# The order of operations in a chunked RWKV-7 core on Trainium2: weight rounding, residual sums, head sums and projection blocks in other places

## The reference, cut to what matters

```python
def rwkv7_step(state, inp):
    r, w, k, v, a, bb = inp
    sa = jnp.einsum('bhij,bhj->bhi', state, a)
    state = (state * w[:, :, None, :] + sa[..., None] * bb[:, :, None, :]
             + v[..., None] * k[:, :, None, :])
    y = jnp.einsum('bhij,bhj->bhi', state, r)
    return state, y
...
    _, y = lax.scan(rwkv7_step, state0, xs)
    y = jnp.moveaxis(y, 0, 1)
    mu = jnp.mean(y, axis=-1, keepdims=True)
    var = jnp.mean(jnp.square(y - mu), axis=-1, keepdims=True)
    y = ((y - mu) * lax.rsqrt(var + GN_EPS)).reshape(b, s, RWKV_WIDTH) * ln_w + ln_b
    bonus = jnp.sum(rh * kh * r_k, axis=-1, keepdims=True) * vh
    return (y + bonus.reshape(b, s, RWKV_WIDTH)) * g
...
        mixed = jnp.concatenate([attn.reshape(b, s, ATTN_WIDTH), rw], axis=-1).astype(h.dtype)
        h = h + mixed @ w_out[l]
```

## Time and profile before

| | us |
|---|---|
| median of 3 runs | 2189.42 (2188.83 to 2189.79) |
| the profiled execution | 2188.19 |
| its span, from the first to the last instruction | 2186.5 |
| TensorE busy | 2125.9 (97%) |
| VectorE busy | 1541.6 (71%) |
| ScalarE busy | 1033.4 (47%) |

### The profile page before, as it was taken

One profiled execution on the slowest core, in us unless ns is written; L12 is line 12 of the kernel. 1 busy time (PEld: TensorE's weight loads), 2 busy tenths in 40 slices (PEclk: granted clock), 3 DMA queues, 4 the chain that ended last, 5 costly groups with the idle time before them and its releaser, 6 DMA issues.

```text
span 2186.5 us, 51663 instructions
## 1 busy us (share of the span) xinstructions
PE 2125.9 (97%) x20608; PEld 2072.9 (95%) x20608; DVE 1541.6 (71%) x2015; ACT 1033.4 (47%) x1342; POOL 267.5 (12%) x178
## 2 busy tenths in 40 slices
PE   7999999999999999999999989899999999999997
PEld 7999999999999999999999888799999999999997
DVE  7889999999645668768877666576666666654544
ACT  6544444444454445556344444654444444444443
POOL 0354444444200000100011000000000000000000
PEclk9999999999999999999999999999999999999999
DMA  7555555555565555555655211255656565556664
GB/s 265 185 171 180 180 182 187 185 184 182 195 193 193 192 201 202 188 184 166 210 180 192 88 51 60 74 188 184 194 192 196 191 195 192 193 187 197 188 191 139
DMA packets 107106, 387.84 MB, mean 177 GB/s; under 512 B 12032, under 2 KB 12160, under 8 KB 106752
## 3 DMA queue, kind: packets, MB, share of 16 engines
q1 hardware_dynamic: 104400, 375.44, 52.5%
q0 software_dynamic: 2176, 9.78, 1.3%
q10 hardware_dynamic: 432, 1.21, 0.1%
HBM read 384.29 MB, written 2.10 MB: 177 GB/s over the span
## 4 chain that ended last, share of the span: by engine, by line
PE 77%; DVE 14%; issue 4%; ACT 3%; DMA 1%; DVEq 0%; SPq 0%; ACTq 0%
PE ps_main L1700 24%; PE ps_main L1701 23%; PE ps_main L1702 23%; DVE w_lo L990 6%; ACT w_hi L503 2%; DVE m L1149 1%; DVE m L1150 1%; PE ps_aux L2055 1%; DVE acc L1156 1%; DMA w_raw<-wmain 1%; DVE g_scan L1159 0%; PE ps_main L2026 0%; PE ps_aux L1942 0%; PE ps_aux L1773 0%; PE ps_main L2027 0%
## 5 line engine op out<-in xcount | busy, mean ns | idle before, releaser
L990 DVE TENSOR_TENSOR w_lo<-w_raw,w_hi 128x1024 fp32r<-128x1024 f32 x718 | 917.8, 1295 | 429.1 <-ACT w_hi L503 421.7
L503 ACT ACTIVATE w_hi<-w_raw 128x1024 fp32r<-128x1024 f32 x718 | 748.4, 1048 | 717.2 <-PE ps_main L1702 656.5
L1700 PE MATMUL ps_main<-xs,w_hi 128*128 128x256 f32 x1664 | 463.2, 278 | 7.7 <-DVE w_lo L990 6.7
L1701 PE MATMUL ps_main<-xs,w_hi 128*128 128x256 f32 x1664 | 460.2, 277 | 0.0
L1702 PE MATMUL ps_main<-xs,w_lo 128*128 128x256 f32 x1664 | 460.2, 277 | 0.0
L1700 PE MATMUL ps_main<-x3s,w_hi 128*128 128x256 f32 x1408 | 389.3, 276 | 0.0
L1701 PE MATMUL ps_main<-x3s,w_hi 128*128 128x256 f32 x1408 | 388.8, 276 | 0.0
L1702 PE MATMUL ps_main<-x3s,w_lo 128*128 128x256 f32 x1408 | 388.8, 276 | 0.0
L1700 PEld LDWEIGHTS ps_main<-xs,w_hi 128*128 128x128 f32 x1664 | 312.8, 188 | 16.1 <-DVE w_lo L990 11.2
L1702 PEld LDWEIGHTS ps_main<-xs,w_lo 128*128 128x128 f32 x1664 | 312.6, 188 | 0.0
L1701 PEld LDWEIGHTS ps_main<-xs,w_hi 128*128 128x128 f32 x1664 | 312.4, 188 | 0.0
(11 more groups left out here) (422 smaller groups left out, 3722.7 us busy)
## 6 DMA issues: line engine op xcount, KB each, us to landing
w_raw<-wmain SPq DMA_DIRECT2D x622, 512.0 KB, 3.5
w_raw<-wdown SPq DMA_DIRECT2D x80, 512.0 KB, 3.7
w_raw<-wdown SPq DMA_DIRECT2D x16, 256.0 KB, 2.7
bias<-bias POOLq DMA_DIRECT2D x8, 384.0 KB, 3.4
x_res<-xt POOLq DMA_DIRECT2D x4, 512.0 KB, 7.2
out<-x_res SPq DMA_DIRECT2D x3, 512.0 KB, 2.8
x_first<-xt SPq DMA_DIRECT2D x2, 512.0 KB, 7.1
x_first<-xt ACTq DMA_DIRECT2D x2, 512.0 KB, 9.9
```

What stands on the lines that cost most here:

```text
L503: nc.scalar.activation(whi[:, s, 0:width], raw[:, s, 0:width], ACT.Copy).then_inc(hi_ready, 1)
L990: V.tensor_tensor(wlo[:, s, 0:width], raw[:, s, 0:width], whi[:, s, 0:width].bitcast(F32), ALU.subtract)\
L1700: nc.tensor.matmul(out, whi[:, s, w], high[:, k, :], start=(first and kk == 0), stop=False)
L1701: nc.tensor.matmul(out, whi[:, s, w], low[:, k, :], start=False, stop=False)
```

## The change

Nothing is added to the arithmetic and nothing is taken from it. Instructions stand in another order, and three results lie in other banks.

- On ScalarE the high part of the unit in the middle of a chunk is rounded ahead of the copy of md, no longer behind it. In chunk 0 the first `wout_hi` stands behind the copy of n4t, no longer ahead of n2t. The copy of x stands behind that of n8.
- On VectorE a residual sum (`wout_add`) now stands ahead of a split (`wout_lo`) in each place: behind n2, behind t1, and at a chunk's end. In the middle of the chunk the split comes right behind the copy of q2. The first split of a chunk stands behind the copy of n4.
- The head sum of the former chunk stands behind the first pair of products and vt, no longer ahead of the pair, and goes to a bank of main (that of the next free column). `centre` follows n2 and a residual sum.
- On TensorE w2 stands ahead of both halves of x, and x's second half behind the pair w4 and n8. w2, w4 and w8 go to B, B and C, x to A.
- TensorE's blocks: 2, 3, 3 in the first part of a chunk become 2, 4, 4 in chunk 0 and, in the others, none, 4, 4 (the second head sum stands in the place of the 2). The product of the gate with y is done ahead of the product with the root (`gated`). The copy of sa stands ahead of `rest`.
- PART goes from (4, 4, 4, 2, 2) to (4, 4, 3, 2, 3): chunk 2 has 24 blocks, no longer 32, and behind the core there are 24, no longer 16. Of these 4 stand ahead of the last head sum, 5 between the two sums and 15 behind; before it was 0, 6 and 10.
- Behind the core the Ln table is loaded (`gg`) ahead of `square`, no longer behind it, and the last low part of the recurrence is made ahead of a split, no longer behind it.

```diff
-        PART = (4, 4, 4, 2, 2)
+        PART = (4, 4, 3, 2, 3)
...
                 exchanged("q", mat["n"])
+                wout_hi()
                 exchanged("md", mat["md"])
-                wout_hi()
...
                 take("n2", mat["n2"])
-                if not i:
-                    gate_bonus(0)
-                wout_lo()
                 if i:
                     wout_add()
-                take("n4", mat["n4"])
+                    centre(i - 1, main[:, first_column(i) % 2, :])
+                    take("n4", mat["n4"])
+                else:
+                    gate_bonus(0)
+                    take("n4", mat["n4"])
+                wout_lo()
...
                 done("t1", V.tensor_tensor(mat["n2t"][:, :, :], mat["nt"][:, :, :], eye, ALU.add))
+                wout_add()
                 if not i:
                     gate_bonus(1)
                 take("q2", mat["n4"])
                 wout_lo()
-                wout_add()
...
+                if i:
+                    c = first_column(i)
+                    pe.wait_ge(wa_free[c % 2], c // 2)
+                    sum_heads(vr[:, :, toks(i - 1)], main[:, c % 2, :])
                 dv("n2")
                 ac("n2t")
                 two(("n4", "n2t", "n2"), ("n4t", "n2", "n2t"))
                 ac("vt")
+                prod("w2", "n2", "w")
+                dv("n4")
                 by_halves(OUT["x"], lambda j, h: (ba[hrow(h), j, toks(i)], state[hrow(h), j, :])).then_inc(x_half, 1)
-                dv("n4")
-                prod("w2", "n2", "w")
-                pe.wait_ge(x_half, i + 1)
-                done("x", second_halves(OUT["x"], lambda j, h: (ga[hrow(1 - h), h, j, :], st[hrow(1 - h), j, h, :])))
                 ac("n4t")
                 dv("w2")
                 two(("w4", "n4", "w"), ("n8", "n4t", "n4"))
-                ac("x")
+                pe.wait_ge(x_half, i + 1)
+                done("x", second_halves(OUT["x"], lambda j, h: (ga[hrow(1 - h), h, j, :], st[hrow(1 - h), j, h, :])))
+                dv("w4")
...
+            wout(4)
             pe.wait_ge(core_act, NCH * len(AC))
             sum_heads(vr[:, :, toks(NCH - 1)], aux[:, 3, :])
-            wout(6)
+            wout(5)
             pe.wait_ge(gn_sq, NCH)
             sum_heads(gsq[:, :, :], aux[:, 2, :])
-            wout(10)
+            wout(15)
```

More of the change, by code:

```diff
@@ L883, in core @@
                 exchanged("n4t", mat["n4t"])
+                if not i:
+                    wout_hi()
+                exchanged("n8", mat["n2"])
                 copy("x", xv)
-                exchanged("n8", mat["n2"])
                 act.wait_ge(core_mm, i * len(MM) + MM["bkt"] + GO)
@@ L911, in core @@
                     .then_inc(core_act, 1)
-                if not last:
-                    wout_hi()
+                for _ in range(PART[i] - 2):
                     wout_hi()
@@ L1437, in masked_products, with diagonal_t @@
                 return V.tensor_tensor(r[:, h, :, :], both[:, :, CH:P], m[:, :, CH:P], ALU.mult)
[L1439 to L1442, removed]
+            def diagonal_t(h):
+                return V.tensor_tensor(mat["nt"][hrow(h), :, :], ga[hrow(h), h, :, :], mask("mdiagt", h), ALU.mult)
             def diagonal(banks):
@@ L1478, in gate_bonus, with centre, gated @@
                     ins.then_inc(gate_mixed, 1)
-            def centre(i):
+            def centre(i, sums):
                 dve.wait_ge(gn_mm, 2 * i + 1)
                 t = vr[:, :, tokens(i)]
-                V.scalar_tensor_tensor(t, aux[:, 3, :].rearrange("p (j n) -> p j n", n=CH), -1.0 / 64, t, ALU.mult, ALU.add)\
+                V.scalar_tensor_tensor(t, sums.rearrange("p (j n) -> p j n", n=CH), -1.0 / 64, t, ALU.mult, ALU.add)\
                     .then_inc(gn_mean, 1)
+            def gated(i):
+                dve.wait_ge(gn_sq, i + 1)
+                for c in range(2):
+                    half = vr[:, 4 * c:4 * c + 4, tokens(i)]
+                    ins = V.tensor_tensor(half, half, gsb[c][:, :, tokens(i)], ALU.mult)
+                link(ins)
             def group_out(i):
@@ L1557, in chunk @@
                 if not last:
+                    diagonal_t(0)
                     mm("g2")
                     done("gm1", masked_products(1, G2, grs[(i + 1) % 2]))
-                    diagonal_t()
+                    diagonal_t(1)
                     mm("n")
                     diagonal(OUT["n"])
-                    done("nf", rest(OUT["n"]))
                 mm("sa")
@@ L1566, in chunk @@
                 if not last:
+                    done("nf", rest(OUT["n"]))
                     done("w1", V.tensor_tensor(mat["w"][:, :, :], mat["nt"][:, :, :], eye, ALU.add))
                     if i:
+                        gated(i - 1)
                         group_out(i - 1)
@@ L2094, in _ @@
                     pe.wait_ge(gate_sb, 4)
-                wout(2)
+                    wout(2)
+                else:
+                    pe.wait_ge(gn_sq, i)
+                    c = first_column(i) + 1
+                    pe.wait_ge(wa_free[c % 2], c // 2)
+                    sum_heads(gsq[:, :, :], main[:, c % 2, :])
                 ac("n8")
+                prod("w8", "n2", "w")
                 if i:
[L2098 to L2102, removed]
+                    pe.wait_ge(gn_mean, i)
+                wout(4)
                 dv("w8")
+                ac("x")
+                two(("qt", "f", "w"), ("q", "w", "f"))
                 if i:
                     pe.wait_ge(gn_var, i)
-                two(("qt", "f", "w"), ("q", "w", "f"))
-                wout(3)
+                wout(4)
                 dv("qt")
@@ L2134, in _ @@
                 done("sa", every_head(OUT["sa"], lambda j, h: (mat["n2"][hrow(h), j, :], xv[hrow(h), j, :])))
-                wout(3 if not last else 2)
+                wout(3 if not last else 1)
                 dv("sa")
```

45 lines of the change are left out of this document (23 added, 22 removed).

## The result

The changed kernel takes 2173.76 us (median; 2172.1 to 2181.3), the kernel before in the same comparison 2189.6: a ratio of 0.9933, 95% interval 0.9921 to 0.9944. The forecast was 2172.9. So 15 to 16 us are gone.

A forecast was written before the change was run, and what follows sets the result against it. TensorE, busy 97%, was taken as the bound, so only waits, switches and clock count: waits 21.4 to 6.9, less 0.6 for switches, plus 1.5 and 1.7 clock, 17.1, taken as 16.5, giving 2172.9 us; range 2170.5 to 2177.

The forecast's parts named there:

- The walk: Prediction's wait-by-wait reckoning of the new order in the stage from 1242 to 1407 us: TensorE's waits from 21.4 to 6.9.
- issue wait: TensorE wait of 0.8 us for "issue", taken as no part of the order and staying; if gone, 0.8 more saved.
- rival (a): The clock falls in chunk 0 behind two new waits, 0.6 and 2.2, costing 1.5 to 1.7: 2174.5 us; chance 0.22.
- m_w in chunk 0: Chunk 0's start: the split waits for w_hi on ScalarE, so TensorE gets a new wait of 2.2 us.
- m_w in chunks 1 to 3: Start of these chunks: w2 before x and a split ahead of m_w; each waits 0.67 where 0.2 stood, 2.0 us.
- rwkv_l: Wait at woutb's start behind the core: chain shorter, more blocks over it, so 3.2 us falls to 0.3.
- m_n4t: Waits in the middle of the chunks: 6.1 us before, 0.1 left in chunk 0 and 0.2 in chunk 3.
- The Ln table ahead of the square: Table load moved earlier behind the core: valued at nothing; by the skill page's figures 0.3 us at most.
- 0.6 for the switches: Head sum between small products in chunks 1 to 3: shape switches cost 0.2 us each, 0.6 in all.
- 1.5 + 1.7: Clock falls regained: 1.5 us in chunk 3 and 1.7 at woutb's start, bringing 13.9 saved to 17.1.
- rival (c): In woutb VectorE leaves more sums and splits behind the core, taking 2 to 3 us back: 2175.5; chance 0.08.
- 16.5 taken: Total saving used for the profiled execution: 17.1 us lowered because the walk came out 0.5 too long on the kernel before.

The follow-up runs named there:

- middle alone: Kernel before with w_hi rounded ahead of md and the residual sum ahead of the copy of q2: ratio 0.9983, distance between the two TensorE marks 168.27 us.
- end alone: Kernel before with PART (4, 4, 3, 2, 3), blocks 4, 5, 15, table and gate products ahead, last low part ahead of a split: ratio 0.9972.
- kernel with the old end: Changed kernel with PART and the blocks (0, 6, 10) as before: 2177.31 us, ratio 0.994.
- split moved in chunk 0 alone: Changed kernel with the first split of a chunk behind w2's sum in chunk 0 only: 2173.93 us, ratio 0.9921.
- version with the split moved: Changed kernel with the split behind the copy of n4 put behind w2's sum in every chunk: 2173.82 us, then 2170.0 with more runs.
- kernel with middle and end: Kernel before with the moves in the middle of a chunk and those behind the core, without the starts of the chunks: 2177.69 us, ratio 0.9937.

## Why the prediction was right, and where it was not

**The bound and the waits: right.** The walk forecast woutb's start near 1391, 1392 with the issue wait; it is at 1392.64 with a fall of the clock in front of it that the forecast left to rival (a). Term by term, forecast and measured: m_n2t in chunk 0 0.6 and 0.50; m_w in chunk 0 2.2 and 2.17; m_w in chunks 1 to 3 0.67 each and 0.61, 0.61, and in chunk 2 an issue wait of 0.5 in its place; stack 0.5 and 0.32; mt's copy, for which sa waits, 0.3 and 0.34; md 0.35 and 0.2; rwkv_l 0.3 and 0.27; m_n4t 0.3 in all and no wait of 0.25 or more. No wait for x_res or rkv, as forecast. (The rows before have 26 waits, where the prediction counts 25; that is worth 0.1.)

**Each part.** That the middle alone takes m_n4t's waits away, that the end alone brings woutb from 3.18 to under 0.5, and that the blocks behind the core cover the copy of y are shown by the experiments. The Ln table ahead of the square was valued at nothing: in the kernel with the old end woutb waits 2.15 where the walk, with nothing for the table, has 2.0. The forecast's 0.6 for the switches was not measured by itself.

**The clock: half right.** "With the clock, 1.5 + 1.7, it is 17.1" took both falls as gone and no new one. Both are gone, and each went with its own wait (middle alone, end alone). But rival (a), given 0.22, is what happened, in all three traces. The argument against it, that waits of 1.4 and 1.5 had not ended in a fall, was weak, since the new wait was 2.2 with one of 0.5 ahead of it, more than the 0.5 and 1.7 of chunk 3 that did. Across the traces: the five with a wait of this size at that place (1.3 with 0.6 for issue, 1.6 with 0.35, 1.9 to 2.2) have the fall; the eight without it (four of them with 1.4 for m_n2t, one with 0.57 left for m_w) have none there. So the fall needs the wait. That it always comes with it is not shown: behind a wait of 2.2 elsewhere in the same kernels it came in eight traces of thirteen (last section). The fall costs about 1.6, an estimate: with the split moved in chunk 0 alone 3.8 were saved, and the wait was 2.2. The Trainium skill (TensorE: Matmul & The Clock Gate, Part 1) says that the moment of a change of clock varies from run to run. The traces agree for that other place: where the clock falls there, it does so between 0.3 before the wait's end and 1.6 behind it; in chunk 0 it is 0.0 to 0.8 behind it.

**woutb: the step that failed.** The sum has 1.7 for the clock at woutb's start and takes the rest of woutb as it was. The 1.7 came in (1.6) and was taken back by the slower spacing of its matmuls, 1.9. It is not rival (c), which had VectorE as the bound: no wait stands there. The forecast had no such case. In the three traces of the changed kernel it is there twice (325 matmuls in 38 us) and once not (337), and it is in none of the other ten traces; so the median of the changed kernel probably holds some of it, and a part of what separates it from the version with the split moved may be that. Whether the order has to do with it, at so few traces, is not settled.

So the number was right within 1 us, in part by luck: the stage without its fall was 0.6 better than forecast (13.9 and 1.5 against 14.8), the fall cost 1.5 and woutb 1.9. The profiled execution gained 13.7, 2.8 less than the 16.5 taken; that the median gained 15.8, 2.1 more than the profiled pair, lies in differences between executions of the same code (last section), which the forecast did not have.

**A better order.** With the split behind w2's sum the distance is 5.4 shorter, in two traces. In the medians it is 2170.0 against 2175.06 on one chip (0.9909 of the kernel before against 0.9928); the comparison on the other chip, of four runs, had 0.9927 and does not show it.

## What to carry over

Where an engine's work can't shrink, write down for each wait the chain that ends it and the work that covers it, and walk the new order before running it: here the distances of nine kernels came out within about 1 us of such a walk, once it was known where the clock falls. A product moved earlier needs its whole chain moved, the other work in its engine's queue included: w2 went ahead of x on TensorE and a split was left in its way on VectorE, which cost 5.4 of the 21 us that were to be had (19.3 in the distance, 1.6 at woutb's start), about 1.6 of them for the clock. Price a new wait of about 2 us with a fall of the clock behind it that is likely though not certain, and compare kernels by a distance between two marks in the trace rather than by medians when a few us are at stake.

## What the runs showed of the hardware that was not expected

**Two spacings of the same matmul.** A 128x256 product of woutb or the large projections starts 113.3 or 117.8 ns behind the one before it at full clock, hardly ever in between, and can keep to one value for hundreds of matmuls. In some places a part of them is slow in every trace, as at 1050 to 1100 us; others are slow only in some traces, as the stretch at 850 to 900 us, where both kernels here have the same code. The version with the split moved, second trace, and the kernel with middle and end:

```profile
850.00:900.00 50.00, 50.00 (x444) 1.00 0.63 201
```
```profile
850.00:900.00 50.00, 50.00 (x427) 1.00 0.60 189
```

The second kernel has 2376 slow steps ahead of the stage where the first has 1416: 960 at 4.5 ns, 4.3 us, in work that no edit touches, and its traced execution took 2181.0 where its median is 2177.7. The three traces with that stretch slow reach the mark at 1236.8 to 1238.3 us, the other ten at 1231.1 to 1235.3. So it is a main part of the spread ahead of the stage; executions without a trace can't be looked into. Inside the distance the same counts are 34 to 156 slow steps, at most 0.6 us of it. What sets the value was not found.

**Falls of the clock behind short waits.** Each fall lasted some 3.4 us at 1.2 GHz; the two that could be priced from differences, in chunk 0 and at woutb's start, cost 1.6 us each. In chunk 0 they followed the wait for m_w (1.3 to 2.2, the shorter ones with an "issue" wait ahead) in five traces of five, and in chunk 3 a wait of 1.7 in two of two; the waits of 1.4 and 1.5 in chunks 0 to 2 were not followed by one. A wait of 3.18 at woutb's start was, both times, and one of 2.15 there, in the kernel with the old end, was not. Near 825 us, in work that no edit touches, all thirteen traces have a wait of 2.2 for the tile ms, and a fall came in eight of them. The version with the split moved, first and second trace:

```profile
824.53 0.38 PE L1714 MATMUL ps_main<-ms,w_hi 128*128 128x256 f32 x1 [2.26 <-DVE ms L1243]
...
826.00:828.00 2.00, 2.00 (x11) 0.50 0.71 236
```
```profile
826.07 0.38 PE L1714 MATMUL ps_main<-ms,w_hi 128*128 128x256 f32 x1 [2.26 <-DVE ms L1243]
...
826.00:828.00 2.00, 1.93 (x14) 1.00 0.79 262
```

The code and the wait are the same, and the clock falls in one execution and not in the other. So a fall can follow a wait of about 2 us and need not; what decides was not tried. Waits of 1.7 to 1.8 near 128 us, in eleven traces, were never followed by one.
